# An encoder layer whose second norm runs on all rows before the last expert tile is added

## The reference, cut to what matters

```python
proj = x @ w_in[l] + b_in[l]                     # conv branch, chunked attention, gates
mixed = (g_conv * y_conv + g_attn * y_attn) @ w_o[l] + b_o[l]
x = layer_norm(ALPHA * x + mixed, ln1_g[l], ln1_b[l])
x = layer_norm(ALPHA * x + grouped_moe(x, w_router, b_router, w_gate_up[l], w_down[l]),
               ln2_g[l], ln2_b[l])

def grouped_moe(h, ...):                         # top-2 experts of 16 for each of 1024 tokens
    for e in range(N_EXPERTS):
        g, u = jnp.split(t @ w_gate_up[e], 2, axis=-1)
        out = out + combine[:, e:e + 1] * ((jax.nn.silu(g) * u) @ w_down[e])
```

## Time and profile before

| what | us |
|---|---|
| median of 3 runs (1199.16 to 1202.43) | 1201.43 |
| the profiled execution, its own time | 1197.6 |
| its span in the trace | 1195.3 |

### The profile page before, as it was taken

One profiled execution on the slowest core, in us unless ns is written; L12 is line 12 of the kernel. 1 busy time (PEld: TensorE's weight loads), 2 busy tenths in 40 slices (PEclk: granted clock), 3 DMA queues, 4 the chain that ended last, 5 costly groups with the idle time before them and its releaser, 6 DMA issues.

```text
span 1195.3 us, 17084 instructions
## 1 busy us (share of the span) xinstructions
PE 1132.2 (95%) x5704; PEld 938.9 (79%) x5705; DVE 816.3 (68%) x1131; ACT 554.8 (46%) x783; POOL 90.0 (8%) x97
## 2 busy tenths in 40 slices
PE   7999999999999999899999999899999999999876
PEld 6888888879777788778888888677788888888653
DVE  5799999735375746566586577697579646558837
ACT  5112121232476745556323134286478545558627
POOL 0000000000000000000000000052122111112200
PEclk9999999999999999999999998999899999999988
DMA  6121333231101010630423236569889866699683
GB/s 251 53 97 36 105 106 89 88 106 56 68 19 41 19 40 1 245 126 35 179 96 157 106 141 233 231 258 372 278 323 382 300 229 200 205 371 353 236 272 141
DMA packets 47573, 198.58 MB, mean 166 GB/s; under 512 B 5136, under 2 KB 5648, under 8 KB 45456
## 3 DMA queue, kind: packets, MB, share of 16 engines
q1 hardware_dynamic: 41600, 176.18, 39.2%
q0 software_dynamic: 5904, 21.50, 7.3%
HBM read 165.68 MB, written 31.98 MB: 165 GB/s over the span
## 4 chain that ended last, share of the span: by engine, by line
PE 76%; DMA 8%; DVE 7%; ACT 5%; issue 3%; ACTq 0%; DVEq 0%; SPq 0%; POOLq 0%
PE ps L450 16%; PE ps L451 16%; PE ps L452 16%; PE ps L1368 7%; PE ps L1370 7%; PE ps L1369 7%; DMA gu<-in_wexp 6%; PE ps L535 1%; PE ps L1436 1%; ACT pth L789 1%; PE ps L1364 1%; PE ps L521 1%; DVE xf L1873 1%; DVE ptl L999 1%; ACT attn L780 1%
## 5 line engine op out<-in xcount | busy, mean ns | idle before, releaser
L450 PE MATMUL ps<-xh,wh 128*128 128x512 f32 x512 | 202.6, 396 | 11.6 <-DVE xl L862 8.1
L451 PE MATMUL ps<-xl,wh 128*128 128x512 f32 x512 | 199.9, 390 | 0.0
L452 PE MATMUL ps<-xh,wl 128*128 128x512 f32 x512 | 199.8, 390 | 0.0
L1282 DVE TENSOR_TENSOR gu<-gu (+1 forms) x128 | 148.6, 1221 | 30.7 <-issue 19.2
L885 DVE SCALAR_TENSOR_TENSOR cv<-u,dw_t,cv 128x1024 f32<-128x1024 f32 x120 | 154.1, 1284 | 3.7
L1368 PE MATMUL ps<-gu,xgh 128*128 x336 | 134.4, 400 | 4.2 <-issue 2.2
L1276 ACT ACTIVATE gu<-gu (+1 forms) x128 | 124.6, 1048 | 23.9 <-DMA gu<-in_wexp 15.5
L1370 PE MATMUL ps<-gu,xgl 128*128 x336 | 132.0, 393 | 0.0
L1369 PE MATMUL ps<-gu,xgh 128*128 x336 | 131.8, 392 | 0.0
L450 PEld LDWEIGHTS ps<-xh,wh 128*128 128x128 f32 x512 | 96.6, 189 | 33.5 <-issue 13.6
L452 PEld LDWEIGHTS ps<-xh,wl 128*128 128x128 f32 x512 | 96.4, 188 | 20.4
(11 more groups left out here) (261 smaller groups left out, 2092.9 us busy)
## 6 DMA issues: line engine op xcount, KB each, us to landing
gu<-in_wexp SPq DMA_DIRECT2D x64, 1024.0 KB, 9.0
dn_raw<-in_wexp SPq DMA_DIRECT2D x16, 2048.0 KB, 10.4
raw<-in_wblk SPq DMA_DIRECT2D x52, 512.0 KB, 3.9
gate_cols<-gst SPq DMA_DIRECT2D x16, 512.0 KB, 5.2
xraw<-in_xT SPq DMA_DIRECT2D x8, 512.0 KB, 7.6
gcm<-gate_cols SPq DMA_DIRECT2D x8, 512.0 KB, 8.5
gam<-gate_cols SPq DMA_DIRECT2D x8, 512.0 KB, 15.4
x<-in_x SPq DMA_DIRECT2D x8, 512.0 KB, 6.2
```

Of the source, the lines that this page charges most:

```text
L450: pe.matmul(o, a_h, b_h, start=first, stop=False)
L451: pe.matmul(o, a_h, b_l, start=False, stop=False)
L452: return pe.matmul(o, a_l, b_h, start=False, stop=last)
L1282: eng.tensor_tensor(gu[:, par, k, 1, :], gu[:, par, k, 1, :].bitcast(F32), gu[:, par, k, 0, :], ALU.subtract).then_inc(gu_lo, 1)
```

## The change: what it does

- **The rows are normed from SBUF, without PE.** ACT takes each piece's total and squares from `xf` itself (the copy goes to `unread`, which nobody reads), and DVE norms `xf` in place. DVE's `scale_row` now also waits for the squares of its piece (`f_sq`), because it overwrites what ACT reads. PE's eight rounds of identity and 0/1 matmuls, `yh`, `yl` and `hot_l` are gone.
- **The last tile's tokens are a ninth piece.** Once the store of `end2` has landed, POOL gathers the `acc_rows` of the last tile's tokens into `rows_l`. DVE adds the scaled output of `down(end1)` to them (`last_rows`), placed between the fourth and the fifth piece, and the ninth piece is normed into `norm_l`. POOL waits for it and for all eight stores of `out` and then writes its rows over `out` by an indirect transfer; slots without a token have an index beyond the last row and are left out by the bounds check. The kernel ends when that has landed.
- **The tail's order changes.** ACT does `h_t(end2)` ahead of `y(end3)`; DVE does it ahead of the split of the down weights of `end2`'s expert. `down(end2)` and `down(end1)` wait for each of the four rows of down weights apart (`by_row`). The split of the last expert's rows is divided around `silu(end1)` on ACT (two and two) and around `gate(end1)` and `h_t(end1)` on DVE (two, one, one).
- **SP** loads the norm's `g2_b` and `b2_b` ahead of the last expert's down weights, and no longer behind them.

```diff
--- before.py
+++ after.py
@@ -184,11 +184,11 @@
-        yh = at("yh", [P, D], F32R, 168)
-        yl = at("yl", [P, D], F32R, 172)
-        xs = at("xs", [P, 3, D], F32, 176)
-        hot_l = at("hot_l", [P, TT, P], F32R, 188)
-        squares = at("squares", [P, D], F32, 56)
+        squares = at("squares", [P, D], F32, 168)
+        rows_l = at("rows_l", [P, D], F32, 172)
+        norm_l = at("norm_l", [P, D], F32, 176)
+        ys2 = at("ys2", [P, D], F32, 180)
+        unread = at("unread", [P, 2, D], F32, 184)

@@ -1252,13 +1252,14 @@
 +            if e == NE - 1:
+                before = sp.value_load(rows_i[0:1, NE - 2:NE - 1], min_val=0, max_val=4 * MAX_TILES - 4)
+                sp.wait_ge(gu_rows, before + 4)
+                sp.dma_start(g2_b[:], ln2_g.partition_broadcast(P)).then_inc(ln2_in, 16)
+                sp.dma_start(b2_b[:], ln2_b.partition_broadcast(P)).then_inc(ln2_in, 16)
             sp.wait_ge(dn_lo, FC * e)
             load_dn(sp, e)
-        before = sp.value_load(rows_i[0:1, NE - 2:NE - 1], min_val=0, max_val=4 * MAX_TILES - 4)
-        sp.wait_ge(gu_rows, before + 4)
-        sp.dma_start(g2_b[:], ln2_g.partition_broadcast(P)).then_inc(ln2_in, 16)
-        sp.dma_start(b2_b[:], ln2_b.partition_broadcast(P)).then_inc(ln2_in, 16)
         end1 = sp.value_load(ends_i[0:1, 1:2], min_val=NE - 1, max_val=MAX_TILES - 1)
         sp.wait_ge(y_out, end1 * 16)
         for t in range(TT):
@@ -1267,6 +1268,7 @@
             sp.wait_ge(f_ok, t + 1)
             sp.dma_start(out[P * t:P * t + P, :], xf[:, t, :]).then_inc(f_out, 16)
         sp.wait_ge(f_out, 16 * TT)
+        sp.wait_ge(last_stored, 1)

@@ -1338,11 +1340,23 @@
         step(2)
         steps(pool, step, end1)
         store(end3)
-        store(end2, xs[:, 2, :])
+        store(end2, ys2[:])
+        pool.wait_ge(gath, total * 16)
+        pool.tensor_copy(to_last[:], to_i[:, bass.ds(end1, 1)]).then_inc(toc, 1)
+        pool.wait_ge(toc, total)
         pool.wait_ge(y_out, end1 * 16)
         pool.sem_inc(id_set, 1)
-        pool.wait_ge(gath, total * 16)
+        pool.indirect_dma_start(out=rows_l[:], out_offset=None, in_=acc_dram,
+                                in_offset=bass.IndirectOffsetOnAxis(ap=to_last[:, 0:1], axis=0)).then_inc(rows_in, 16)
+        pool.wait_ge(f_ok, TT + 1)
+        pool.wait_ge(f_out, 16 * TT)
         pool.sem_inc(id_set, 1)
+        pool.indirect_dma_start(out=out, out_offset=bass.IndirectOffsetOnAxis(ap=to_last[:, 0:1], axis=0),
+                                in_=norm_l[:], in_offset=None, bounds_check=SEQ - 1, oob_is_err=False).then_inc(y_out, 16)
+        pool.wait_ge(y_out, total * 16)
+        pool.sem_inc(last_stored, 1)

@@ -1461,13 +1475,16 @@

-        def down(i):
+        def down(i, by_row=False):
             e = load(pe, T_E, i)
             pe.wait_ge(th_lo, i + 1)
-            pe.wait_ge(dn_lo, e * FC + FC)
+            if not by_row:
+                pe.wait_ge(dn_lo, e * FC + FC)
             if not (isinstance(i, int) and i == 0):
                 pe.wait_ge(y_ok, i)
             for k in range(FC):
+                if by_row:
+                    pe.wait_ge(dn_lo, e * FC + (k + 1))
                 for h in range(2):
                     c = slice(HALF * h, HALF * h + HALF)
                     last = mm3(pe, ps[:, 6 + h, :], hbh[:, P * k:P * k + P], hbl[:, P * k:P * k + P],
@@ -1518,28 +1535,10 @@
         par = load(pe, T_PAR, end1)
         pe.wait_ge(tx_lo, total)
         up_rows(NE - 1, bass.ds(par, 1), range(KC // 2))
-        down(end2)
+        down(end2, by_row=True)
         up_rows(NE - 1, bass.ds(par, 1), range(KC // 2, KC))
         transpose_h(end1)
-        down(end1)
-        for t in range(TT):
-            bank = 2 * (t % 3)
-            pe.wait_ge(row_in[t], 32)
-            if t >= 3:
-                pe.wait_ge(f_tot, t - 2)
-            for h in range(2):
-                c = slice(HALF * h, HALF * h + HALF)
-                pe.matmul(ps[:, bank + h, :], ident, xf[:, t, c], start=True, stop=False)
-            if t == 0:
-                pe.wait_ge(last_hot, TT)
-                pe.wait_ge(yh_ok, 1)
-                pe.wait_ge(yl_ok, 1)
-            for h in range(2):
-                c = slice(HALF * h, HALF * h + HALF)
-                pe.matmul(ps[:, bank + h, :], hot_l[:, t, :], yh[:, c], start=False, stop=False)
-                last = pe.matmul(ps[:, bank + h, :], hot_l[:, t, :], yl[:, c], start=False, stop=True)
-            last.then_inc(f_sum, 1)
+        down(end1, by_row=True)

@@ -1563,7 +1562,7 @@
                 act.wait_ge(gu_rows, 4 * i)
             act.activation((xgh2 if isinstance(i, int) and i == 1 else xgh)[:], psf[:, 0:SEQ], ACT.Copy).then_inc(tx_hi, 1)
-        def down_rows(i, first=False, before=None):
+        def down_rows(i, first=False, before=None, rows=range(FC)):
             e = 0 if first else load(act, T_E, i - 1)
             act.wait_ge(dn_in, e * 16 + 16)
             if first:
...
@@ -1620,30 +1619,31 @@
             step(i)
         steps(act, step, end1)
         x_t(end1)
+        h_t(end2)
         y(end3)
         when(act, T_SPLIT_DN, end1, None, lambda: down_rows(end1, before=end2))
-        h_t(end2)
-        y(end2, xs[:, 2, :], False)
-        when(act, T_SPLIT_DN, total, None, lambda: down_rows(total, before=end1))
+        y(end2, ys2[:], False)
+        when(act, T_SPLIT_DN, total, None, lambda: down_rows(total, before=end1, rows=range(2)))
         silu(end1)
+        when(act, T_SPLIT_DN, total, None, lambda: down_rows(total, before=end1, rows=range(2, FC)))
         h_t(end1)
-        act.wait_ge(w_set, 1)
-        act.wait_ge(dn_done, total)
-        act.activation(yh[:], psf[:, 6 * HALF:8 * HALF], ACT.Copy, scale=w_last[:]).then_inc(yh_ok, 1)
         def total_of(t):
-            act.wait_ge(f_sum, t + 1)
-            if t >= 3:
-                act.wait_ge(f_g, t - 2)
-            act.activation(xs[:, t % 3, :], psf[:, 2 * HALF * (t % 3):2 * HALF * (t % 3) + D], ACT.Copy,
-                           accum_out=mv[:, t, 0:1]).then_inc(f_tot, 1)
+            if t < TT:
+                act.wait_ge(row_in[t], 32)
+                rows = xf[:, t, :]
+            else:
+                act.wait_ge(rows_ok, 1)
+                rows = rows_l[:]
+            act.activation(unread[:, t % 2, :], rows, ACT.Copy, accum_out=mv[:, t, 0:1]).then_inc(f_tot, 1)
         total_of(0)
-        for t in range(TT):
-            if t + 1 < TT:
+        for t in range(TT + 1):
+            if t < TT:
                 total_of(t + 1)
             act.wait_ge(f_nm, t + 1)
-            act.activation(squares[:], xs[:, t % 3, :], ACT.Square, bias=nmr[:, t:t + 1], accum_out=mv[:, t, 1:2]).then_inc(f_sq, 1)
+            act.activation(squares[:], xf[:, t, :] if t < TT else rows_l[:], ACT.Square, bias=nmr[:, t:t + 1],
+                           accum_out=mv[:, t, 1:2]).then_inc(f_sq, 1)
             act.wait_ge(f_sq, t + 1)
             act.activation(rstd[:, t:t + 1], mv[:, t, 1:2], ACT.Sqrt, scale=1.0 / D, bias=eps2[:]).then_inc(f_sd, 1)
...
@@ -1842,19 +1842,14 @@
         steps(dve, step, end1)
         x_t(dve, end1)
         late_rows(end2)
+        h_t(end2)
         when(dve, T_SPLIT_DN, end1, None, lambda: down_rows(end1))
-        h_t(end2)
         dve.tensor_copy(w_last[:], w_slot[:, bass.ds(end1, 1)]).then_inc(w_set, 1)
-        link(V.tensor_copy(to_last[:], to_i[:, bass.ds(end1, 1)]))
-        for t in range(TT):
-            dve.tensor_scalar(hot_l[:, t, :], iota, float(P * t), to_last[:], ALU.add, ALU.is_equal).then_inc(last_hot, 1)
-        when(dve, T_SPLIT_DN, total, None, lambda: down_rows(total))
+        when(dve, T_SPLIT_DN, total, None, lambda: down_rows(total, rows=range(2)))
         gate(end1)
+        when(dve, T_SPLIT_DN, total, None, lambda: down_rows(total, rows=range(2, FC - 1)))
         h_t(end1)
-        dve.wait_ge(w_set, 1)
-        dve.wait_ge(yh_ok, 1)
-        dve.scalar_tensor_tensor(out=yl[:], in0=psf[:, 6 * HALF:8 * HALF], scalar=w_last[:], in1=yh[:],
-                                 op0=ALU.mult, op1=ALU.subtract).then_inc(yl_ok, 1)
+        when(dve, T_SPLIT_DN, total, None, lambda: down_rows(total, rows=range(FC - 1, FC)))
         def mean(t):
             dve.wait_ge(f_tot, t + 1)
@@ -1862,21 +1857,34 @@
         def scale_row(t):
             dve.wait_ge(f_nm, t + 1)
-            dve.scalar_tensor_tensor(out=xf[:, t, :], in0=xs[:, t % 3, :], scalar=nmr[:, t:t + 1], in1=g2_b[:],
-                                     op0=ALU.add, op1=ALU.mult).then_inc(f_g, 1)
+            if t < TT:
+                dve.wait_ge(f_sq, t + 1)
+            dve.scalar_tensor_tensor(out=xf[:, t, :] if t < TT else norm_l[:], in0=xf[:, t, :] if t < TT else rows_l[:],
+                                     scalar=nmr[:, t:t + 1], in1=g2_b[:], op0=ALU.add, op1=ALU.mult).then_inc(f_g, 1)
         def finish(t):
+            rows = xf[:, t, :] if t < TT else norm_l[:]
             dve.wait_ge(f_sd, t + 1)
```

(18 more changed lines are left out.)

17 lines of the change are left out of this document (9 added, 8 removed).

## The result

| | median us | executions |
|---|---|---|
| kernel before | 1200.3 | 4, from 1197.59 to 1202.43 |
| changed kernel | 1189.2 | 4, from 1188.55 to 1190.16 |
| ratio, with its 95% interval | 0.992 | [0.9899, 0.994] |

The changed kernel is faster by 11.1 us in these medians. The profiled execution took 1189.55 us with a span of 1187.4; before it was 1197.6 and 1195.3, a difference of 8.05 us.

The account below looks back on a forecast made before the run. It took the end to be bound by the last tile, then the sum over PE, then eight pieces at DVE's pace. -14.9 + 4.45 + 4.0 = -6.5 took 1197.6 to 1191.1, plus 3.8 to the median: 1194.9 us, range 1191 to 1200.5.

Parts of the forecast that it names:

- The sum: Whole change: norm starts 14.9 us earlier, gains 4.45 in length, the end costs 4.0 more; together -6.5 us.
- it is 3.8 us under the median, so the median goes to 1194.9 us: Last step: profiled execution of before, 1197.6 us, goes to 1191.1; adding its 3.8 us distance from the median gives 1194.9.
- 4.85 us earlier: Tail on PE: `down(end2)` ends at 1139.15 instead of 1144.0, 3.15 us from the gap and 1.7 from the clock.
- The landing of the store: POOL's store of `end2`, beside the load of the last down weights: taken to land in 7.5 us, against 6.4 uncrowded.
- crowded store: Rival: the store of `end2` meets the down weights' load and takes 11.0 us; +3.5, 1198.4, no measurable change; chance 0.11.
- The end: Behind the ninth piece: eighth store, POOL's issue, scatter of 5.3 us and hop to SP cost +4.0 us over the plain store.
- the scatter decides: Rival: POOL's final scatter takes over 15.4 us and turns the sign; at 19.7 us it gives 1209.3, slower; chance 0.06.
- They cost it at most 2.8 us, and ACT wants it at 1129.5: nothing: Early vectors, 1 MB at about 1119.8, delay the load of expert 14's down weights by at most 2.8 us, at no cost.
- the head: Tail's part up to `down(end2)`: `hbl` made ahead of the `dn_l` rows, waits row by row; `down(end2)` ends 4.85 us earlier.
- the row-by-row wait: At `down(end2)`: PE goes on at 1133.7 without a gap, 1.37 us per `k` against DVE's 1.155 per row.
- the one-time price of `f_sq`: In the norm: DVE waits for ACT's squares once, +0.63 us, since its 2.65 us per piece exceeds ACT's 2.46.
- the unhindered `last_rows`: In the norm: `last_rows` costs +1.2 us without idle time ahead, last down product and gather being hidden by pieces 0 to 3.

Follow-up runs that it names:

- e7: The changed kernel, but with the norm's two vectors loaded behind the last down weights as before: 1192.55 us, ratio 0.9951.
- e4: The changed kernel, but with the old order of the tail and the two vectors late, so only the norm is new: 1194.65 us, ratio 0.9966.

## Why the prediction was right and where it was wrong

The sum was right, partly by errors that cancel, and what it was added to was wrong. By the forecast's own steps, against the trace of the changed kernel. That execution reached its last gather at 1100.30 and the one of before at 1101.73, so the last column adds these 1.43 us to every time; it is the one to compare with the forecast, which reckoned from the trace of before.

| step | forecast | measured | from the same last gather |
|---|---|---|---|
| `down(end2)` starts | 1133.7 | 1133.82 | 1135.25 |
| `y(end2)` starts | 1139.45 | 1139.70 | 1141.13 |
| store of `end2` issued | 1141.35 | 1141.59 | 1143.02 |
| its landing | 7.5 | 6.06 | |
| second total starts | 1153.45 | 1152.26 | 1153.69 |
| wait for squares, once | 0.63 | 0.70 | |
| eighth piece done | 1179.15 | 1178.19 | 1179.62 |
| ninth piece done | 1181.75 | 1180.78 | 1182.21 |
| scatter issued | 1182.8 | 1181.76 | 1183.19 |
| its landing | 5.3 | 3.3 | |
| from landing to the span's end | 0.6 | 2.3 | |
| span | 1188.7 | 1187.4 | 1188.8 |

**The step that failed is the last one: "it is 3.8 us under the median, so the median goes to 1194.9 us".** The median was that of three executions, 1201.43; thirty others have 1197.87, and the later sets 1199.15 and 1198.38. The profiled execution of before lay 0.3 us under the thirty's median, not 3.8. -6.5 from 1197.9 is 1191.4, and the changed kernel measured 1190.3 over seven executions and 1189.2 over four. The range then carried the same error: its lower end assumed a good start of 1.5 us under a centre that was itself up to 3.5 us too high. The rest of the miss is small and partly the luck of four executions: for the profiled execution the forecast said 1191.1 and it took 1189.55, and 1.43 of these 1.55 us lie ahead of the last gather, where the change does nothing. Against the ratio of the larger set, 0.9946 or -6.5 us (by its interval -3.8 to -9.2), the sum of the forecast is met, and against the mean of the tails, -7.2, it is 0.7 short.

**`down(end2)`, "4.85 us earlier"** was mis-sized. Counted from the last gather it started 33.52 us later instead of 35.12, which is 1.6 us earlier and not 3.15; with the full speed of its matmuls the store of `end2` was issued 3.2 us earlier and not 4.84. What took the rest was the place of the vectors: with them late, in e7, the store was issued 39.33 us behind the last gather, 5.1 us earlier than the 44.46 of before.

**The landing of the store** was mis-sized by 1.4 us, which is why the norm started when it should although the store came late: these two cancel by luck. I put the crowding by the load of the weights at 1.1 us and it was next to nothing: the load landed at 1144.5, and the store's rows moved only from 1143.7 on. The rival "crowded store" did not happen, but e7 shows its mechanism with a price of 2.8 us as soon as the vectors are queued there.

**The end** had two errors that cancel. The scatter landed in 3.3 us, below the 4.2 that I took as the quickest transfer of its kind. The Trainium skill's fit (DMA: Bandwidth & Descriptors, Anatomy of one DMA — SWDGE (gpsimd) path) gives 3.2 us for 512 KB and, as an estimate, 3.1 us for the 459 KB that were moved, and the trace agrees within 0.3 us; its warning about a long completion when the target is HBM did not show. The rival "the scatter decides" needed 15.4 us. Against that, 2.0 us of POOL's drain were missing in the sum: "0.4 us as now" was read from an end whose last actor was SP.

**"They cost it at most 2.8 us, and ACT wants it at 1129.5: nothing"** was the wrong cover. I looked at who waits for the weights of expert 14 and not at who else uses the DMA engines then. Early vectors cost some 2 us at the entry of the tail (4.48 against 2.24 to 2.62 us) and save 2.8 at the store (6.07 against 8.84 in e7); at the last weights they save nothing that the runs show (7.3 us in e7 too). The net is in favour of the change, 1.0 us in the last column and 2.2 by the medians of one set, and `down(end2)` started where I said only because in this execution the loop was left 1.7 us sooner than in the first trace (silu of `end2` at 1120.16 against 1121.83). Of the 4.5 us that the head is worth in the last column (91.4 to 86.9) the order of the engines brings 3.5 (e4 to e7, 87.9) and the place of the vectors 1.0.

**Right for their reasons** were the row-by-row wait (idle time ahead of `down(end2)` 0.77 us instead of 3.14, and its matmuls all 0.23 us apart, where before seven stood 0.43 apart), the one-time price of `f_sq`, the unhindered `last_rows`, the eighth store landing just behind the ninth piece, and that norm and last tile hardly overlap: the first piece was finished at 1157.7, the last down product at 1159.0. What makes the change pay is not overlap but a shorter way to the first total.

## What to carry to other kernels

Cost a change against one trace and take its base from many executions: three executions put the base up to 3.5 us too high here, about half of the whole effect, and set traces side by side from an event that both share, here the last gather. When a load is moved into a quiet place, ask for every user of the DMA engines there, by the reading below the instruction queues among them, and not only for the next reader of the data. A last step given to POOL's indirect transfers cost its landing and another 2 us of drain here; it is worth it only where it takes more than that out of the chain, as in this kernel.

## What the runs showed of the hardware that I had not expected

Where the loop over tiles is left, ACT and DVE stand still, for a part of the time with nothing in the profile to wait for. On DVE this took 2.24 to 2.62 us in the six traces whose vectors are loaded late or in the gap, and 4.40 to 4.72 in the seven where 1 MB is queued at 1115 to 1120, with the old code and with the new. The page counts the instruction queues among the transfers of the same engines:

```profile
q8 instruction: 41, 0.67, 0.2%
...
q14 instruction: 29, 0.23, 0.1%
```

Shown is that moving the vectors alone, in either kernel, moves the stall by 2 us. That it is the tail's code that comes late behind the vectors is a reading, and the packets of q14 speak for it: the first two of them after the loop is left lie 0.7 to 1.1 us apart in the six traces and 1.9 to 2.3 in the seven.

POOL's drain at the end of the program took 2.03 us with its scatter landed and 5.36 us with the scatter just issued. And the indirect store of 459 KB without addition landed in 3.3 us in every kernel that has it, while the adding ones of 512 KB took 6.1 to 6.4 at best.
